# Second attention: the mean square by two float32r products, its root and scaling one slot on

## The reference

```
s1 = q1 k1^T * scale;  s2 = q2 k2^T * scale            # rotated halves of 64, masked in chunks of 64
a  = softmax(s1) - lam * softmax(s2)
o  = a v
o  = o * rsqrt(mean(o * o, axis=-1) + 1e-5)            # over the 128 values of a head
o  = o * subln_g * (1 - lambda_init);  x @ w_out after it
```

## Time and profile before

| | |
|---|---|
| median of 3 runs | 1830.65 us (1828.85 to 1831.72) |
| profiled execution, its own time | 1829.41 us |
| its span in the trace | 1827.6 us |
| PE busy | 1791.4 us, 98% of the span |
| PE weight loads | 1491.7 us, 82% |
| POOL busy | 1032.5 us, 56% |
| ACT busy | 783.1 us, 43% |
| DVE busy | 732.3 us, 40% |
| the chain that ended last | PE 90%, DVE 4%, ACT 2%, POOL 1%, issue 1%, DMA 1% |

### The profile page before, as it was taken

How to read it: one execution, slowest core, us unless ns; L and a number is a source line. 1 busy time by engine, 2 the same in 40 slices (tenths; PEclk the granted TensorE clock), 3 DMA queues, 4 the chain that set the end, 5 groups by cost and what they waited for, 6 DMA issues and landing times.

```text
span 1827.6 us, 26879 instructions
## 1 busy us (share of the span) xinstructions
PE 1791.4 (98%) x8816; PEld 1491.7 (82%) x8816; DVE 732.3 (40%) x1346; ACT 783.1 (43%) x1622; POOL 1032.5 (56%) x927
## 2 busy tenths in 40 slices
PE   8999999999999999999999999989999999999997
PEld 6889888888887888788888888878887888888886
DVE  7964000001235556453333322456664533333224
ACT  5434323232235556464444422545564644444221
POOL 6856655665562333466666654656554666666551
PEclk9999999999999999999999999999999999999999
DMA  5312333323234554323333233333332233332332
GB/s 151 93 35 82 104 97 98 92 78 112 86 89 112 133 136 111 92 76 100 101 92 97 82 104 90 76 81 93 86 82 62 70 106 102 92 103 78 104 90 97
DMA packets 327251, 171.93 MB, mean 94 GB/s; under 512 B 43458, under 2 KB 316948, under 8 KB 327188
## 3 DMA queue, kind: packets, MB, share of 16 engines
q1 hardware_dynamic: 327172, 171.12, 33.5%
q10 hardware_dynamic: 16, 0.00, 0.0%
HBM read 152.15 MB, written 2.10 MB: 84 GB/s over the span
## 4 chain that ended last, share of the span: by engine, by line
PE 90%; DVE 4%; ACT 2%; POOL 1%; issue 1%; DMA 1%; SPq 1%; DVEq 0%; ACTq 0%; POOLq 0%
PE bank L952 24%; PE bank L954 24%; PE bank L953 24%; PE attended L952 2%; PE attended L954 2%; PE attended L953 2%; PE turned L1372 1%; PE attended L1388 1%; DVE small L2367 1%; ACT pmap L1798 1%; PE bank L1053 1%; PE bank L1041 1%; PE score L1354 1%; DVE xres L2096 1%; PE score L1356 1%
## 5 line engine op out<-in xcount | busy, mean ns | idle before, releaser
L721 POOL TENSOR_TENSOR WL<-raw,WH 128x512 fp32r<-128x512 f32 (+3 forms) x656 | 776.7, 1206 | 583.8 <-ACT WH L1551 582.9
L952 PE MATMUL bank<-XL,WH 128*128 128x512 f32 (+1 forms) x1440 | 571.7, 397 | 2.8 <-POOL WL L721 1.2
L954 PE MATMUL bank<-XH,WL 128*128 128x512 f32 (+1 forms) x1440 | 560.6, 389 | 0.0
L953 PE MATMUL bank<-XH,WH 128*128 128x512 f32 (+1 forms) x1440 | 560.2, 389 | 0.0
L1551 ACT ACTIVATE WH<-raw 128x512 fp32r<-128x512 f32 (+3 forms) x656 | 338.3, 565 | 305.0 <-PE bank L954 193.9
L954 PEld LDWEIGHTS bank<-XH,WL 128*128 128x128 f32 x1440 | 270.8, 188 | 57.2
L952 PEld LDWEIGHTS bank<-XL,WH 128*128 128x128 f32 x1440 | 271.3, 188 | 55.8 <-issue 1.2
L953 PEld LDWEIGHTS bank<-XH,WH 128*128 128x128 f32 x1440 | 271.5, 189 | 50.7
L952 PE MATMUL bank<-HL,WH 128*128 128x512 f32 (+1 forms) x528 | 200.6, 380 | 0.0
L953 PE MATMUL bank<-HH,WH 128*128 128x512 f32 (+1 forms) x528 | 200.3, 379 | 0.0
L954 PE MATMUL bank<-HH,WL 128*128 128x512 f32 (+1 forms) x528 | 200.3, 379 | 0.0
(11 more groups left out here) (344 smaller groups left out, 2504.7 us busy)
## 6 DMA issues: line engine op xcount, KB each, us to landing
raw<-in_ffn_w_in SPq DMA_DIRECT2D x88, 512.0 KB, 3.7
raw<-in_w_gate SPq DMA_DIRECT2D x22, 512.0 KB, 3.7
raw<-in_w_up SPq DMA_DIRECT2D x22, 512.0 KB, 3.7
raw<-in_ffn_w_out SPq DMA_DIRECT2D x28, 384.0 KB, 3.2
raw<-in_ffn_w_out SPq DMA_DIRECT2D x28, 320.0 KB, 3.2
raw<-in_a_w_in SPq DMA_DIRECT2D x16, 512.0 KB, 4.0
raw<-in_kv_w SPq DMA_DIRECT2D x32, 256.0 KB, 3.1
raw<-in_w_in SPq DMA_DIRECT2D x12, 512.0 KB, 3.8
```

What stands on the lines that cost most here:

```text
L721: pool.tensor_tensor(wl, x, wh, ALU.subtract).then_inc(w_lo, 1)
L952: pe.matmul(out_, wh, xl, start=start, stop=False)
L953: pe.matmul(out_, wh, xh, start=False, stop=False)
L954: return pe.matmul(out_, wl, xh, start=False, stop=stop)
```

## The change

The squares of a head are now written twice by ACT, as float32 (`osq`) and rounded to float32r (`sq_h`, in a free part of PTH), and POOL makes their rest `sq_l = osq - sq_h` (in PTL). PE sums both with ones taken as float32r: two products in place of one float32 matmul. This holds for the heads of the first seven units; the last one, summed while "out2" is woven in, keeps the float32 matmul. Mean square and root go from slot 2 to slot 3, the scaling on DVE from slot 3 to 4, the rounding on ACT from slot 4 to 5. On ACT the root now stands behind `exps(2)`, and the rounding behind `exps(5)`, as before behind `exps(4)`.

```
         QHZ, QLZ = (x[:, 1, 0:2 * S].rearrange("p (c s) -> p c s", c=2) for x in (PTH, PTL))
+        sq_h, sq_l = (x[:, 1, 2 * S:3 * S] for x in (PTH, PTL))
...
+            def square_low(u):
+
+                pool.wait_ge(sub_sq, u.n(1))
+                pool.wait_ge(sub_top, u.n(1))
+                pool.tensor_tensor(sq_l[:, :], osq[:, :], sq_h[:, :].bitcast(F32), ALU.subtract).then_inc(sub_rest, 1)
...
+                if not first_unit(au):
+                    square_low(au + -1)
                 if iu is None:
                     low(Nth(STAGES["out2"][0] + 2))
                 else:
...
-                    if sl == 2 and not (isinstance(u.it, int) and u.base == 0):
+                    if sl == 3 and not first_unit(u):
                         mean_square(u + -1)
...
             def mean_square(u):
 
-                pe.wait_ge(sub_sq, u.n(1))
-                pe.matmul(ob[1][:, :], ones[:, :], osq[:, :], start=True, stop=True).then_inc(sub_var, 1)
+                if last_unit(u):
+                    pe.wait_ge(sub_sq, u.n(1))
+                    pe.matmul(ob[1][:, :], ones[:, :], osq[:, :], start=True, stop=True).then_inc(sub_var, 1)
+                    return
+                pe.wait_ge(sub_rest, u.n(1))
+                pe.matmul(ob[1][:, :], ones[:, :].bitcast(F32R), sq_h[:, :], start=True, stop=False)
+                pe.matmul(ob[1][:, :], ones[:, :].bitcast(F32R), sq_l[:, :], start=False, stop=True).then_inc(sub_var, 1)
...
                     if sl == 2:
                         value_hi(1, au)
-                        if before is not None:
-                            sub_root(before)
+                    if sl == 3 and before is not None:
+                        sub_root(before)
...
-                    if sl == 4 and before is not None:
+                    if sl == 5 and before is not None:
                         sub_high(before)
...
                         act.activation(osq[:, :], ob[0][:, :], ACT.Square).then_inc(sub_sq, 1)
+                        if iu is not None:
+                            act.activation(sq_h[:, :], ob[0][:, :], ACT.Square).then_inc(sub_top, 1)
                         act.activation(osb[:, :], ob[0][:, :], ACT.Copy).then_inc(o_read[0], 1)
...
-                    if sl == 3 and not first_unit(au):
+                    if sl == 4 and not first_unit(au):
                         head_scaled(au + -1)
```

More of the change, by code:

```diff
@@ L395, in two_blocks @@
             sem(x) for x in ("sub_sq", "sub_var", "sub_ln", "sub_rs", "sub_n", "sub_hi", "sub_lo"))
+        sub_top, sub_rest = sem("sub_top"), sem("sub_rest")
         y_turned = sem("y_turned")
```

## The result

| | before | after |
|---|---|---|
| median | 1828.85 us (5 runs, 1826.91 to 1831.72) | 1841.52 us (5 runs, 1836.77 to 1842.44) |
| ratio | | 1.0058, 95% interval 1.0045 to 1.0072 |
| span of the profiled execution | 1827.6 us | 1839.7 us |
| PE busy | 1791.4 us | 1794.1 us |

What follows compares the result with a forecast made beforehand. The prediction took PE's own work to bound the kernel; six steady units at +0.9 (-0.40 + 1.1 + 0.2) give +5.4, the last unit -0.2, together +5.2 us, hence 1835.8, range 1828.2 to 1842.0.

Steps and rivals of the forecast that it cites:

- PE bounds the unit, the mean square gives back 0.40: PE's work sets the unit; two float32r products cost 0.46 for 0.85, gaining 0.40 in each of seven units, 2.8 us.
- The added square and rest are hidden: ACT's extra square and POOL's extra subtraction cost nothing, with 0.5 and 1.3 us of cover (POOL's 0.8 after a late unit).
- The scaling is put on DVE's full chain, POOL's queue follows the late rounding: Scaling (0.74) makes DVE some 0.7 late; POOL's queue meets the second combination; PE's transpose waits 1.1, next first score 0.2.
- the unit of the prediction: The steady unit of the kernel before, starting at 1249.15 us, whose times the prediction uses.
- the second combination: DVE's 128x384 combination, read by a PE transpose; predicted to run 1265.95 to 1266.55, where it ended at 1264.83 before.
- They take turns, and the waiting one starts 0.2 before the recorded end: DVE work with both inputs in SBUF and POOL work exclude one another; the waiter starts 0.2 before the other's recorded end.
- Rival D: Chance 0.10: exclusion lasts to the recorded end, each of three turns up to 0.2 later; unit +1.4, sum +8.2, 1838.9.
- The third combination keeps its turn: DVE's third combination, at about 1268.9, goes ahead of POOL's large weight rests at about 1269.0, a lead of 0.1.
- rival B: Chance 0.20: POOL's weight rests go before the third combination, 1.26 more to the chain; unit +2.0, sum +11.8, 1842.4.
- The forecast's own unit: Steady unit in the main forecast: -0.40 gained by PE, +1.1 and +0.2 of waits, sum +0.9.
- the likeliest case: The main forecast, chance 0.35: +5.2 us in all, 1835.8, with its own range of 1833 to 1838.
- The last unit, -0.2: No rope work, PE saves 0.40, its 0.7 of waits roughly stays: -0.2, bounds -1.1 and +1.3.

Runs made afterwards that it cites:

- e1: Changed kernel with the float32 mean square as before, without second square and rest, the changed order kept; 1844.92 us, ratio 1.0079.
- e4: Changed kernel with the scaling back in DVE's slot 3 and the rounding back in ACT's slot 4; 1827.5 us, ratio 0.9984.
- e6: Kernel before plus the second square on ACT and a same-size subtraction on POOL, neither used; 1830.8 us in one run.
- e12: e4 with the last unit's rounding of the second output weights on ACT moved from slot 5 to 10; 1827.94 us, ratio 0.9988.
- e7: Changed kernel plus three unused one-column copies on ACT ahead of the rounding of the next unit's first weights; 1833.34 us, ratio 1.0019.
- e2: Changed kernel with only the scaling back in DVE's slot 3; 1834.8 us, ratio 1.0028.
- e3: Changed kernel with only the rounding back in ACT's slot 4; 1837.2 us, ratio 1.0040.
- e11: Changed kernel with the rounding back in ACT's slot 4 and three unused one-column copies on ACT; 1828.8 us in one run.

## Why the prediction was right, and where it was off

- **PE bounds the unit, the mean square gives back 0.40**: right. 0.47 for two products in place of 0.85, 0.39 a unit from e1 to the changed kernel, 25.16 a unit in e4.
- **The added square and rest are hidden**: right, e4 and e6.
- **The scaling is put on DVE's full chain, POOL's queue follows the late rounding**: right to a tenth. In the unit of the prediction the rounding was put at 1261.2 and came at 1261.18, the head's rest 1261.9 and 1261.99, the rope sum's end 1266.1 and 1266.05, the second combination's end 1266.55 and 1266.47, the transpose's wait 1.1 and 1.05 (1266.52 for 1265.47). The scaling itself was held too: 1.26 us for 0.74.
- **They take turns, and the waiting one starts 0.2 before the recorded end**: right. The held 128x384 combination ended at 1270.08, so with its 0.62 of the earlier trace rows it began at 1269.46; the rope sum's recorded end is 1269.66. Rival D's mechanism is not what these rows show. It is the hold to the recorded end, as the Trainium skill (page "SBUF — State Buffer", § SBUF: two separate sides) would give it if read so; the blocking that the page states is in these rows, 1.52 us for 0.62.
- **The third combination keeps its turn**: wrong, and this is the step that set the size. I had DVE's instruction at 1268.9 and POOL's at 1269.0, a lead of 0.1. They came at 1268.83 and 1268.85, and POOL went first, in all six units. A lead of 0.1 might well have been enough: with 0.12 to 0.15 the turn was kept in all twelve steady units of e4 and e12. It was the lead itself that was mis-sized, by the start of POOL's rests, for which the prediction shows no sum. They wait for ACT's rounding of the weights (WH), which stands behind its rounding of the third transposed map (PTH). ACT in the kernel before, then in the changed kernel:

```profile
1266.39 0.49 ACT L1803 ACTIVATE PTH<-turned 128x384 fp32r<-128x384 f32 x1 [0.15 <-PE turned L1372]
1266.78 1.14 ACT L1551 ACTIVATE WH<-raw 128x512 fp32r<-128x512 f32 x2
```

```profile
1270.71 0.69 ACT L1813 ACTIVATE pmap<-score,small 128x512 f32<-128x512 f32 x1 [0.39 <-DVE small L2384]
1271.39 0.48 ACT L1818 ACTIVATE PTH<-turned 128x384 fp32r<-128x384 f32 x1
1271.76 1.15 ACT L1566 ACTIVATE WH<-raw 128x512 fp32r<-128x512 f32 x2
```

  Before, the last exponentials started at 1265.46 and PE's third transpose at 1265.87, so ACT waited for the transpose, and the rounding of the weights started 1.32 behind the exponentials. In the change the transpose (1270.13) comes ahead of the exponentials (1270.71), ACT waits for nothing, and that distance is 1.05. DVE's combination starts 1.73 behind the exponentials in both. So the lead goes from 0.29 to 0.02. In e4 the transpose starts 0.24 behind the exponentials, and the lead is 0.12. The kernel before had such a case in its trace: in its first unit with attention, where ACT does not wait for the transpose either, the turn is lost:

```profile
1215.68 1.84 DVE L2497 SCALAR_TENSOR_TENSOR pmap<-pmap,small 128x512 f32<-128x512 f32 x1
```

```profile
1215.71 2.96 POOL L721 TENSOR_TENSOR WL<-raw,WH 128x512 fp32r<-128x512 f32 x2 [1.23 <-ACT WH L1551]
```

  What came is rival B (0.20): +2.0 a unit foreseen for it and +1.96 measured, 1842.4 and 1841.5. Its split fits less well. Its waits as printed, 1.1, 0.3 and 0.8, less the 0.40, make 1.8 and not 2.0; by the starts on PE the third transpose is delayed by 1.05, the fourth by 0.4 to 0.5, the product of maps and values by 0.3, for which B had nothing, and the first score by 0.6. The forecast's own unit is what the kernel shows once the turn is given back: +0.9 foreseen, 26.49 - 25.56 = +0.93 in one unit of e7. (The whole of e7 is only +3.5, 1.8 to 5.3, for the forecast's +5.2. Its copies give back the lost turn of the first attention unit too.) The measured change is twice the forecast and outside the likeliest case's own range of 1833 to 1838. That it lies in the stated range, 0.5 under its upper end, is owed to the weight given to B and not to the forecast.
- **The last unit, -0.2**: right, by 31.95 against 32.17.

The chances should have been nearer to even between the forecast and B: a lead of 0.1 at the end of a long chain of rows can't decide an order, and an error of 0.08 turned it.

## What to carry to other kernels

When PE never waits, look at how near the others are before moving work by a slot: the same 0.74 us of scaling was free ahead of one instruction, and behind it cost 0.9 us a unit with the late rounding (e2 against the changed kernel) and 1.4 to 2.5 without it (e4 against e3). When DVE and POOL both work on SBUF, put the two queues side by side and mark each pair within a few tenths; such a pair is worth one whole instruction of the other engine, and can be turned by work as small as 0.4 us on a third one. Ask of each such pair what sets the distance: here it was a wait of ACT for PE, and it vanished when DVE became late. Undo a change part by part; here its gain stood, and two of its moves had to go back.

## What the runs showed of the hardware that I had not expected

- A lead of 0.02 or 0.03 us of DVE's recorded start over POOL's does not win the turn (1272.44 against 1272.46 in the changed kernel, 1268.66 against 1268.68 in e2, 1215.68 against 1215.71 in the kernel before). 0.12 to 0.15 does (e4, e12), and so do 0.20 (e3) and 0.31 (e7). The recorded starts thus do not tell who comes first: either DVE's lies ahead of the moment at which it excludes POOL, or POOL's behind its own; these runs can't say which.
- In six units of one execution the same turn went the same way each time; units that differ only in being written out behind a loop went the other way, with POOL's start 0.2 us earlier against DVE's (e3, e11).
- POOL's clearing of 128x512 values took 0.53 us beside DVE, its subtraction of the same size 1.26 to 1.30.
